# MoE slots filled by an indirect DMA from a DRAM copy of the normed rows, in place of a selection matmul

## The chip, the cores and the metric

One core of a Trainium2 chip runs the program. The metric is device time in microseconds of one execution. The kernel before takes 1042.7 us, the median of 3 runs (1040.01 to 1045.47).

## The reference, cut to what matters

One inference step of two layers over 320 token rows of 1024 features (256 of a new stream, 64 of a running one). Layer 0 uses differential attention, layer 1 forgetting attention; each ends with a mixture of experts (MoE), all in float32. Only the MoE bears on this change:

```python
def hier_moe(t, w_group, b_group, w_expert, b_expert, w_gate, w_up, w_down):
    # one of 4 groups per token, then the 2 best of its 4 experts: gates is (n, 16), 2 nonzero a row
    ...
    for e in range(N_EXPERTS):                       # 16 experts
        hid = jax.nn.silu(t @ w_gate[e]) * (t @ w_up[e])      # (1024, 512) each
        y = y + gates[:, e:e + 1] * (hid @ w_down[e])         # (512, 1024)
    return y
```

`t` is the RMS-normed residual. The weights of one layer's experts are 16 x 3 matrices of 2 MB.

## The kernel before, in words

Rows lie on partitions in three tiles of 128 (the last has 64 real rows). `x` is the residual, `h2` the normed rows that enter the MoE. Semaphores written out by hand set the order on every engine; each engine runs its instructions in program order.

**Routing.** PE computes the router's logits from `h2T` (L1291), VectorE (DVE) picks two experts per row in a chain of some 20 small dependent operations (L1773 to L1788) that ends in the 0/1 matrix `sel`. PE sums `sel` over earlier rows (L1316 to L1326), so each token gets a rank inside its expert. Each expert has CAP = 64 slots. `build_pick` (L1792) compares ranks with 1..64 and makes `pick`, the 0/1 selection matrix (token row x slot) of four experts; its first half is ready before its second (`pick_ready`). `stay_busy(bank, n)` (L971) issues n float32 matmuls of 128x256 on constants, each two instructions, whose result nobody reads.

**Gather.** Experts are worked on in MPAIRS = 8 pairs, two experts of 64 slots filling 128 partitions. `gather(i)` (L1329) multiplies `pick` by the rows: ScalarE (ACT) has split `h2` into a rounded part `h2_hi` (L887) and DVE into the rest `h2_lo` (L1758), and 12 matmuls of 128x512 per pair add both over three tiles. ACT and DVE copy the result to `x_slots` (L897, L1825), `transpose_slots` (L1344) turns it, and both copy it to `xT` (`slots_T`).

**A pair's work on PE**, in this order (L1411 to L1444): `into(i, "g", 0)`, the gate product (32 matmuls); `gather(i + 1)`; `into(i, "u", 1)`, the up product (32); `back(i - 1, (0,))`; `transpose_slots(i + 1)`; four transposes of `hid`; `back(i - 1)` for the other tiles, which scatters the previous pair's outputs through `pickT` and which DVE adds to `x` (L1848); `slots(i + 1)`, which transposes `pick` and picks the gates; `down(i)`, the down product (32).

**Weights.** SyncE (SP) loads the experts' weights in units of 1 MB, 12 for a pair and 96 for a layer, each half of a matrix, in the order in which PE uses them (`load_experts`, L481). There are 15 places for a unit: w_raw (6), w_more (4), w_extra (5). `plan()` (L109) gives each unit a place, and SP waits at L470 until the unit that held it before has been used (`units_used`). In layer 0 the loads of four units of layer 1's input projection (fox_w_in) stand in the same queue before pair 6's down weights (L485 to L487), and fewer places are open to the last 28 units (L149 to L150).

**GpSimd (POOL)** issues the small loads, the stores of keys and values, and computes the inverse roots of the norms (`rms`, L551). In the MoE it has nothing to do.

The overflow branch (more than 64 tokens at an expert) is not entered with these inputs.

Of the kernel before, what the change touches and what calls it, by code (L numbers as in the profile page):

```python
# [22 lines left out]
F32 = mybir.dt.float32  # L23
F32R = mybir.dt.float32r
# [5 lines left out]
P = 128  # L30
# [33 lines left out]
BACK = [3, 0, 5]  # L64

# [4 lines left out]
C_WIDTH = C_PRIO + EXPERTS + 1  # L70
# [5 lines left out]
def constants():  # L76
# [11 lines left out]
    c[:, C_PRIO:C_PRIO + EXPERTS] = np.arange(EXPERTS, 0, -1)  # L88
    dist = np.zeros((P, BIAS), np.float32)
# [72 lines left out]
def build(nc, A):  # L162
    with ExitStack() as ctx:
# [124 lines left out]
        const_r = sb("const_r", [P, 3 * P], F32R, offset=gain_at + 4 * D)  # L288
        before_r, ones_r = const_r[:, 0:P], const_r[:, 2 * P:3 * P]
# [5 lines left out]
        h2_lo = sb("h2_lo", [P, TILES, D], F32R, offset=h_at)  # L295
        h2_hi = sb("h2_hi", [P, TILES, D], F32R, offset=qk_at)
# [34 lines left out]
        def link(eng, which, ins):  # L331
# [19 lines left out]
            sq1=3, rstd1=3, h_ready1=3, tr1=6, ev1=6, h2hi=4, h2lo=3, logits=1, logit_sb=2, gexp=2, selected=1, ranks=2,  # L351
            routed=1, pick_ready=5, gathered=16, slots_act=8, slots_dve=8, slots_tr=16, x_act=8, x_dve=8, pT_done=8, pickT_ready=8, slot_gated=8, silu_done=8,
# [170 lines left out]
        def _(pool):  # L523
# [35 lines left out]
            for l in range(2):  # L559
# [89 lines left out]
                rms(B, "sq1", "rstd1")  # L649

# [11 lines left out]
        def _(act):  # L662
# [9 lines left out]
            for l in range(2):  # L672
# [213 lines left out]
                for t in range(TILES):  # L886
                    A_(h2_hi[:, t, :], h2[:, t, :], ACT.Copy).then_inc(L["h2hi"], 1)  # L887
                A_(const_r[:, :], cst[:, C_BEFORE:C_BEFORE + 3 * P], ACT.Copy).then_inc(L["h2hi"], 1)
# [5 lines left out]

                def copy_slots(i):
                    act.wait_ge(L["gathered"], B["gathered"] + 2 * i + 1)
                    A_(x_slots[:, 0:F], ps[:, 5, :], ACT.Copy).then_inc(L["slots_act"], 1)  # L897
# [17 lines left out]
                copy_slots(0)  # L915
                slots_T(0)
                copy_pickT(0)
                for i in range(MPAIRS):
# [5 lines left out]
                    if i + 1 < MPAIRS:  # L924
                        copy_slots(i + 1)
                        slots_T(i + 1)
                    elif l == 0:

                        split_hi(IN[1][0])
                        split_hi(IN[1][1])  # L930
# [31 lines left out]
        def _(pe):  # L962
# [66 lines left out]
            for l in range(2):  # L1029
# [286 lines left out]
                for t in range(TILES):  # L1316
                    out = ps[:, 7, EXPERTS * t:EXPERTS * (t + 1)]
                    if t == 0:
                        pe.wait_ge(L["h2hi"], B["h2hi"] + 4)
# [7 lines left out]
                pe.wait_ge(L["h2lo"], B["h2lo"] + TILES)  # L1327

                def gather(i):  # L1329

                    pe.wait_ge(L["pick_ready"], B["pick_ready"] + (1 if i == 0 else i // 2 + 2))
                    if i >= 3:
                        pe.wait_ge(L["x_added"], B["x_added"] + 3 * (i - 2))
                    elif i >= 1:
                        pe.wait_ge(L["x_act"], B["x_act"] + i)
                        pe.wait_ge(L["x_dve"], B["x_dve"] + i)
                    cols = slice(i % 2 * P, i % 2 * P + P)
                    for c in range(2):
                        for t in range(TILES):
                            mm(ps[:, 5 + c, :], pick[:, t, cols], h2_hi[:, t, c * F:(c + 1) * F], start=(t == 0), stop=False)  # L1340
                            ins = mm(ps[:, 5 + c, :], pick[:, t, cols], h2_lo[:, t, c * F:(c + 1) * F], start=False, stop=(t == TILES - 1))  # L1341
                        ins.then_inc(L["gathered"], 1)
# [596 lines left out]
```

## Time and profile before

| | |
|---|---|
| median of 3 runs | 1042.7 us |
| the profiled execution | 1042.3 us, its span 1040.5 us |
| PE busy | 974.9 us, 94% of the span, 4789 matmuls |
| DVE, ACT, POOL busy | 434.9, 312.9, 113.6 us |
| chain that ended last | PE 85%, DVE 7%, ACT 3%, DMA 2% |
| of it the gather's two lines, L1340 and L1341 | 3% and 2% |
| DMA | 260.30 MB, mean 250 GB/s, of which SP's queue 242.64 MB |

The span is one execution. "Busy" is the time in which an engine ran an instruction; for PE, ends are modelled, so a busy PE need not be at its peak. The chain is followed back from the last instruction: at each step to what released it. DMA share is the mean busy share of 16 DMA engines. A row of the chain reads: start in us, duration in us, what.

### The profile page before, as it was taken

Reading aid. Unit: us, or ns where it says so; the run is one execution under the profiler, and the core shown is the slowest. Engines: PE = TensorE matmul, PEld = TensorE weight load, DVE = VectorE, ACT = ScalarE, POOL = GpSimd, SP = SyncE. Lnnn points to the kernel's source line nnn. Section 1 sums busy time; section 2 is a strip of 40 time slices with the busy share of each in tenths; the row PEclk is TensorE's granted clock in tenths of the full one; section 3 lists DMA queues with packets and bytes.
Section 4 is the critical chain, followed back from the end, with each engine's and each line's share of the span. In section 5 each row is a group of like instructions: output and inputs, shape, how many; then the busy total and the mean of one; then the engine's idle time right before and its main releaser. Section 6 shows DMA issues by size and latency. Waiting matters only on the chain.

```text
span 1040.5 us, 12144 instructions
## 1 busy us (share of the span) xinstructions
PE 974.9 (94%) x4789; PEld 609.8 (59%) x4789; DVE 434.9 (42%) x883; ACT 312.9 (30%) x612; POOL 113.6 (11%) x148
## 2 busy tenths in 40 slices
PE   4999999898999999988989999999798999999997
PEld 3777666686444444433767777776687444444443
DVE  4666467435122312227366525465625122213223
ACT  4544667323111111124244433343313111111110
POOL 5234123200000000001213310100000000000000
PEclk9999989899999999999899999999799999999999
DMA  9735612534999999997233521311555899999991
GB/s 294 267 122 176 196 43 60 196 149 186 368 421 421 421 421 420 357 420 265 81 122 102 192 80 31 107 45 52 204 232 231 328 420 419 421 422 420 420 414 58
DMA packets 53339, 260.30 MB, mean 250 GB/s; under 512 B 5088, under 2 KB 5328, under 8 KB 28704
## 3 DMA queue, kind: packets, MB, share of 16 engines
q1 hardware_dynamic: 47824, 242.64, 59.0%
q0 software_dynamic: 5456, 16.83, 5.4%
q8 instruction: 42, 0.69, 0.3%
q14 instruction: 17, 0.14, 0.0%
HBM read 252.88 MB, written 6.57 MB: 249 GB/s over the span
## 4 chain that ended last, share of the span: by engine, by line
PE 85%; DVE 7%; ACT 3%; DMA 2%; issue 1%; POOL 1%; SPq 0%; DVEq 0%; POOLq 0%
PE ps L1375 21%; PE ps L1391 11%; PE ps L967 7%; PE ps L968 6%; PE ps L969 6%; PE ps L1340 3%; PE ps L1341 2%; PE ps L1404 2%; PE ps L1020 2%; PE ps L1021 2%; PE ps L1196 2%; PE ps L1405 2%; PE ps L1136 2%; PE ps L1192 2%; PE ps L1350 1%; PE ps L1122 1%
## 5 line engine op out<-in xcount | busy, mean ns | idle before, releaser
L1375 PE MATMUL ps<-w_raw,xT 128*64 128x512 f32 x408 | 174.1, 594 | 0.4 <-issue 0.4
L1375 PE MATMUL ps<-w_extra,xT 128*64 128x512 f32 x376 | 131.5, 594 | 4.0 <-DMA w_raw<-in_moe_w_gate 1.3
L1491 DVE TENSOR_TENSOR w_lo<-w_raw,w_hi 128x2048 fp32r<-128x2048 f32 x36 | 82.1, 2288 | 44.6 <-ACT w_hi L670 44.5
L967 PE MATMUL ps<-w_hi,hT_hi 128*128 128x512 f32 x224 | 94.7, 423 | 3.8 <-DVE w_lo L1491 3.1
L1391 PE MATMUL ps<-w_raw,hidT 128*64 128x512 f32 x216 | 96.0, 595 | 0.0
L968 PE MATMUL ps<-w_lo,hT_hi 128*128 128x512 f32 x224 | 90.2, 403 | 0.0
L969 PE MATMUL ps<-w_hi,hT_lo 128*128 128x512 f32 x224 | 90.1, 402 | 0.0
L1375 PEld LDWEIGHTS ps<-w_extra,xT 128*64 128x64 f32 x376 | 40.8, 137 | 82.3 <-issue 82.3
L1375 PE MATMUL ps<-w_more,xT 128*64 128x512 f32 x240 | 88.4, 593 | 0.0
L670 ACT ACTIVATE w_hi<-w_raw 128x2048 fp32r<-128x2048 f32 x36 | 68.4, 1910 | 42.0 <-PE ps L1021 39.3
L1391 PE MATMUL ps<-w_extra,hidT 128*64 128x512 f32 x184 | 71.1, 595 | 0.0
L1848 DVE TENSOR_TENSOR x<-x,ps 128x1024 f32<-128x1024 f32 x48 | 57.0, 1219 | 12.6 <-PE ps L1405 12.6
L1825 DVE COPY x_slots<-ps 128x512 f32<-128x512 f32 x16 | 11.1, 692 | 118.5 <-PE ps L1341 118.5
L1843 DVE TENSOR_TENSOR y_lo<-ps,y_hi 128x512 fp32r<-128x512 f32 x32 | 22.1, 692 | 90.7 <-ACT y_hi L913 90.6
L1375 PEld LDWEIGHTS ps<-w_raw,xT 128*64 128x64 f32 x408 | 53.0, 137 | 10.3 <-issue 10.3
L1375 PEld LDWEIGHTS ps<-w_more,xT 128*64 128x64 f32 x240 | 27.2, 137 | 53.7 <-issue 53.7
L1872 DVE SCALAR_TENSOR_TENSOR hid<-hid,slot_gate,ps 128x512 f32<-128x512 f32 x16 | 12.0, 747 | 103.9 <-PE ps L1375 103.9
L967 PEld LDWEIGHTS ps<-w_hi,hT_hi 128*128 128x128 f32 x224 | 43.4, 194 | 15.2 <-DVE w_lo L1491 3.5
L901 ACT ACTIVATE xT<-ps 128x512 f32<-128x512 f32 x16 | 9.6, 598 | 134.7 <-PE ps L1350 134.7
L1391 PE MATMUL ps<-w_more,hidT 128*64 128x512 f32 x112 | 49.7, 595 | 0.1
L969 PEld LDWEIGHTS ps<-w_hi,hT_lo 128*128 128x128 f32 x224 | 43.3, 193 | 10.3
L968 PEld LDWEIGHTS ps<-w_lo,hT_hi 128*128 128x128 f32 x224 | 43.5, 194 | 8.3
(290 smaller groups left out, 1771.1 us busy)
## 6 DMA issues: line engine op xcount, KB each, us to landing
w_extra<-in_moe_w_up SPq DMA_DIRECT2D x28, 1024.0 KB, 13.0
w_raw<-in_moe_w_gate SPq DMA_DIRECT2D x27, 1024.0 KB, 10.6
w_raw<-in_moe_w_down SPq DMA_DIRECT2D x27, 1024.0 KB, 11.2
w_raw<-in_moe_w_up SPq DMA_DIRECT2D x24, 1024.0 KB, 12.4
w_extra<-in_moe_w_down SPq DMA_DIRECT2D x23, 1024.0 KB, 13.2
w_extra<-in_moe_w_gate SPq DMA_DIRECT2D x19, 1024.0 KB, 11.7
w_more<-in_moe_w_gate SPq DMA_DIRECT2D x18, 1024.0 KB, 12.8
w_raw<-in_fox_w_in SPq DMA_DIRECT2D x16, 1024.0 KB, 5.4
```

Of the source, the lines that this page charges most:

```text
L670: A_(w_hi[:, U.hslot, :], w_raw[:, U.slot, :], ACT.Copy).then_inc(hi_ready, 1)
L967: mm(out, a_hi, b_hi, start=start, stop=False)
L968: mm(out, a_hi, b_lo, start=False, stop=False)
L969: return mm(out, a_lo, b_hi, start=False, stop=stop)
L1020: mm(acc(b, t), a_hi[:, kb, ts], hi[:, k, :], start=(kb == 0), stop=False)
L1021: ins = mm(acc(b, t), a_hi[:, kb, ts], lo[:, k, :], start=False, stop=(kb == KB - 1))
L1340: mm(ps[:, 5 + c, :], pick[:, t, cols], h2_hi[:, t, c * F:(c + 1) * F], start=(t == 0), stop=False)
L1375: ins = mm(ps[j * CAP:(j + 1) * CAP, bank, :], xT[:, i % 2, kb, j * CAP:(j + 1) * CAP], buffer(U.slot)[:, k * F:(k + 1) * F], start=(kb == ...
L1391: ins = mm(ps[j * CAP:(j + 1) * CAP, 3 + c, :], hidT[:, fb, j * CAP:(j + 1) * CAP], buffer(U.slot)[:, k * D + c * F:k * D + (c + 1) * F], ...
L1491: v.tensor_tensor(w_lo[:, U.slot, :], w_raw[:, U.slot, :], w_hi[:, U.hslot, :].bitcast(F32), ALU.subtract).then_inc(lo_ready, 1)
L1843: v.tensor_tensor(y_lo[:, cs], ps[:, 3 + c, :], y_hi[:, cs].bitcast(F32), ALU.subtract).then_inc(L["y_lo"], 1)
L1848: v.tensor_tensor(x[:, t, :], x[:, t, :], ps[:, BACK[t]:BACK[t] + 2, :].rearrange("p b n -> p (b n)"), ALU.add).then_inc(L["x_added"], 1)
```

## The change: what it does

Per layer, POOL stores the three tiles of `h2` to a DRAM buffer `h2_rows` when each is normed. Constants get a column pair per tile with the value 383 - row. `row_sums(i)` multiplies `pick` by them (3 matmuls, 2 columns), so that each slot gets 383 minus its token's row, or 0 when it is empty; DVE turns that into an integer row number (383 for an empty slot; that row of the padded tile is zero). POOL then gathers 128 rows of 4 KB from `h2_rows` into `x_slots` by one indirect DMA for each pair. `h2_hi`, `h2_lo`, the 12 matmuls, and the copies to `x_slots` go. `transpose_slots(i + 1)` moves into the middle of `down(i)`. Ahead of the first pair two `stay_busy(4, 8)` are put around `slots(0)`.

```diff
+    c[:, C_ROW:C_ROW + 2 * TILES:2] = NO_ROW - (np.arange(TILES)[None] * P + i[:, None])   # NO_ROW = 383
...
+        rows_r = sb("rows_r", [P, TILES, 2], F32R)
+        slot_row = sb("slot_row", [P, 2], I32)
+        h2_rows = [nc.dram_tensor(f"h2_rows{i}", (TILES * P, D), F32, kind="Internal").ap() for i in range(2)]
-        h2_lo = sb("h2_lo", [P, TILES, D], F32R, offset=h_at)
-        h2_hi = sb("h2_hi", [P, TILES, D], F32R, offset=qk_at)
...                                                             GpSimd
                 rms(B, "sq1", "rstd1")
+                for t in range(TILES):
+                    pool.wait_ge(L["h_ready1"], B["h_ready1"] + t + 1)
+                    pool.dma_start(h2_rows[l][t * P:(t + 1) * P, :], h2[:, t, :]).then_inc(L["h2_stored"], 16)
+                pool.wait_ge(L["h2_stored"], B["h2_stored"] + 16 * TILES)
+                for i in range(MPAIRS):
+                    pool.wait_ge(L["slot_rows"], B["slot_rows"] + i + 1)
+                    if i == 0:
+                        pool.wait_ge(L["ranks"], B["ranks"] + 2)
+                    else:
+                        pool.wait_ge(L["slots_tr"], B["slots_tr"] + 2 * i)
+                    pool.indirect_dma_start(x_slots[:, :], None, h2_rows[l][:, :], bass.IndirectOffsetOnAxis(ap=slot_row[:, i % 2:i % 2 + 1], axis=0)).then_inc(L["rows_landed"], 16)
...                                                             ScalarE
-                for t in range(TILES):
-                    A_(h2_hi[:, t, :], h2[:, t, :], ACT.Copy).then_inc(L["h2hi"], 1)
+                A_(rows_r[:, :, :].rearrange("p t n -> p (t n)"), cst[:, C_ROW:C_ROW + 2 * TILES], ACT.Copy).then_inc(L["consts_r"], 1)
...
-                copy_slots(0)
+                copy_pickT(0)
                 slots_T(0)
...
-                    if i + 1 < MPAIRS:
-                        copy_slots(i + 1)
-                        slots_T(i + 1)
...
                     if i + 1 < MPAIRS:
                         copy_pickT(i + 1)
+                        slots_T(i + 1)
...                                                             TensorE
-                def gather(i):
+                def row_sums(i):
                     pe.wait_ge(L["pick_ready"], B["pick_ready"] + (1 if i == 0 else i // 2 + 2))
...
-                            mm(ps[:, 5 + c, :], pick[:, t, cols], h2_hi[:, t, c * F:(c + 1) * F], start=(t == 0), stop=False)
-                            ins = mm(ps[:, 5 + c, :], pick[:, t, cols], h2_lo[:, t, c * F:(c + 1) * F], start=False, stop=(t == TILES - 1))
+                    out = ps[:, ROWS_BANK[min(i, 1)], 0:2]
+                    for t in range(TILES):
+                        ins = mm(out, pick[:, t, i % 2 * P:i % 2 * P + P], rows_r[:, t, :], start=(t == 0), stop=(t == TILES - 1))
+                    ins.then_inc(L["row_sums"], 1)
                 def transpose_slots(i):
-                    pe.wait_ge(L["slots_act"], B["slots_act"] + i + 1)
-                    pe.wait_ge(L["slots_dve"], B["slots_dve"] + i + 1)
+                    pe.wait_ge(L["rows_landed"], B["rows_landed"] + 16 * (i + 1))
+                    if i >= 2:
+                        pe.wait_ge(L["x_added"], B["x_added"] + 3 * (i - 1))
...
                 def down(i):
                     pe.wait_ge(L["hT_copied"], B["hT_copied"] + i + 1)
                     for half in range(2):
+                        if half == 1 and i + 1 < MPAIRS:
+                            transpose_slots(i + 1)
...
-                gather(0)
+                row_sums(0)
+                stay_busy(4, 8)
+                slots(0)
+                stay_busy(4, 8)
                 transpose_slots(0)
-                slots(0)
...
                     into(i, "g", 0)
                     if i + 1 < MPAIRS:
-                        gather(i + 1)
+                        row_sums(i + 1)
...
                     if i + 1 < MPAIRS:
-                        transpose_slots(i + 1)
+                        pe.wait_ge(L["slot_rows"], B["slot_rows"] + i + 2)
...                                                             VectorE
-                low_parts(0)
-                low_parts(1)
...
-                low_parts(2)
...
                 build_pick(0)
+                def slot_rows(i):
+                    dve.wait_ge(L["row_sums"], B["row_sums"] + i + 1)
+                    v.tensor_scalar(slot_row[:, i % 2:i % 2 + 1], ps[:, ROWS_BANK[min(i, 1)], 0:1], -1.0, float(NO_ROW), ALU.mult, ALU.add).then_inc(L["slot_rows"], 1)
+
+                slot_rows(0)
```

On DVE `slot_rows(i + 1)` takes the place of `copy_slots(i + 1)`, and `slots_T(i + 1)` moves behind `take_gates(i + 1)`.

## Rows read from the trace of the kernel before

**Rows 1.** The page: busy tenths in 40 slices of 26 us, PE and DMA.
```profile
PE   4999999898999999988989999999798999999997
DMA  9735612534999999997233521311555899999991
```

**Rows 2.** Windows, two pairs: us; busy PE, PEld, DVE, ACT, POOL; PEclk, DMA share, GB/s.
```profile
343.72:372.54 28.82, 28.82 (x140) 13.15 (x138) 7.29 (x11) 4.08 (x7) 0.00 (x0) 1.00 1.01 421
...
861.68:890.49 28.81, 28.81 (x141) 13.16 (x138) 7.22 (x10) 4.08 (x7) 0.00 (x0) 1.00 1.01 420
```

**Rows 3.** DMA by queue, 8 to 30 us: packets, MB, share of 16 engines.
```profile
q1 hardware_dynamic: 2458, 4.92, 62.0%
q0 software_dynamic: 910, 2.84, 39.8%
```

**Rows 4.** The chain of waits, one pair of layer 0: the gather's first matmul, then up.
```profile
290.74 0.43 PE ps L1340
...
293.71 7.02 PE ps L1375 x32
```

**Rows 5.** The chain of waits, end of the MoE of layer 0.
```profile
460.45 11.11 DMA w_extra<-in_moe_w_up
...
478.86 7.07 PE ps L1391 x32
```

**Rows 6.** Windows in pair 5 of layer 0, where DMA drops.
```profile
422.00:424.00 2.00, 2.00 (x12) 0.58 (x10) 0.09 (x1) 0.00 (x0) 0.00 (x0) 1.00 0.60 246
424.00:426.00 2.00, 2.00 (x12) 0.72 (x10) 0.00 (x0) 0.00 (x0) 0.00 (x0) 1.00 0.42 53
426.00:428.00 2.00, 2.00 (x12) 0.70 (x10) 0.69 (x1) 0.60 (x1) 0.00 (x0) 1.00 0.74 283
```

**Rows 7.** Window in which layer 1's last weights arrive.
```profile
1014.00:1016.00 2.00, 2.00 (x12) 0.62 (x10) 0.00 (x0) 0.00 (x0) 0.00 (x0) 1.00 0.33 131
```

**Rows 8.** The chain of waits, end of the MoE of layer 1.
```profile
1019.55 0.43 PE ps L1404
...
1023.08 7.07 PE ps L1391 x32
```

**Rows 9.** Timeline ahead of layer 0's first pair: start, us, engine, line.
```profile
239.84 1.96 PE L1294 MATMUL ps<-w_router,h2T 128*128 128x20 f32 x16
240.77 2.36 DVE L1758 TENSOR_TENSOR h_lo<-h,h_hi 128x1024 fp32r<-128x1024 f32 x2 [5.32 <-ACT h_hi L887]
241.65 4.56 PE L975 MATMUL ps<-cst 128*128 128x256 f32 x20
243.04 0.21 DVE L1773 TENSOR_TENSOR router<-ps,b_router 128x60 f32<-128x60 f32 x1
...
247.77 0.21 DVE L1787 TENSOR_TENSOR sel<-router,cst 128x48 fp32r<-128x48 f32 x1
...
248.73 0.48 PE L1325 MATMUL ps<-sel,const_r 128*128 128x16 f32 x3
...
249.34 1.03 DVE L1799 TENSOR_TENSOR pick<-router,cst 128x384 fp32r<-128x384 f32 x2
...
252.73 0.21 DVE L1821 TENSOR_TENSOR gates_hl<-router,gates_hl 128x48 fp32r<-128x48 f32 x1
...
255.46 1.13 PE L1350 MATMUL ps<-cst,x_slots 128*128 128x128 f32 x8 [0.88 <-DVE x_slots L1825]
...
257.42 3.65 PE L1375 MATMUL ps<-w_raw,xT 128*64 128x512 f32 x16 [0.19 <-issue]
```

**Rows 10.** Window within it.
```profile
250.00:254.00 4.00, 3.96 (x11) 3.18 (x12) 2.56 (x14) 0.60 (x1) 0.00 (x0) 0.58 0.00 0
```

**Rows 11.** DMA issues: queue, count, KB each, median us from issue to landing.
```profile
w_raw<-in_fox_w_in SPq DMA_DIRECT2D x16, 1024.0 KB, 5.4
...
gain<-in_norm_mix POOLq DMA_DIRECT2D x1, 512.0 KB, 12.3
...
mask<-in_c_mask POOLq DMA_DIRECT2D x1, 480.0 KB, 3.8
```

More of the change, by code:

```diff
@@ L64 @@
 BACK = [3, 0, 5]
+ROWS_BANK = [3, 2]
 C_ID, C_IOTA, C_TRI, C_BEFORE, C_AFTER, C_ONE = (i * P for i in range(6))
@@ L69 @@
 C_PRIO = C_VALID + TILES
-C_WIDTH = C_PRIO + EXPERTS + 1
+C_ROW = C_PRIO + EXPERTS
+NO_ROW = TILES * P - 1
+C_WIDTH = C_ROW + 2 * TILES
 KEYS = [128, 256, 576]
@@ L350, in build @@
             o_hi=6, o_lo=6, out_done=2, low_out_moved=1, x_mid=3,
-            sq1=3, rstd1=3, h_ready1=3, tr1=6, ev1=6, h2hi=4, h2lo=3, logits=1, logit_sb=2, gexp=2, selected=1, ranks=2,
-            routed=1, pick_ready=5, gathered=16, slots_act=8, slots_dve=8, slots_tr=16, x_act=8, x_dve=8, pT_done=8, pickT_ready=8, slot_gated=8, silu_done=8,
+            sq1=3, rstd1=3, h_ready1=3, tr1=6, ev1=6, consts_r=2, h2_stored=48, logits=1, logit_sb=2, gexp=2, selected=1, ranks=2,
+            routed=1, pick_ready=5, row_sums=8, slot_rows=8, rows_landed=128, slots_tr=16, x_act=8, x_dve=8, pT_done=8, pickT_ready=8, slot_gated=8, silu_done=8,
             hid_done=8, hT_done=8, hT_copied=8, y0_done=16, y_hi=16, y_lo=16, back_done=24, x_added=24)
@@ L885, in _ @@
                 copy_h2T(2)
-                for t in range(TILES):
-                    A_(h2_hi[:, t, :], h2[:, t, :], ACT.Copy).then_inc(L["h2hi"], 1)
-                A_(const_r[:, :], cst[:, C_BEFORE:C_BEFORE + 3 * P], ACT.Copy).then_inc(L["h2hi"], 1)
+                A_(const_r[:, :], cst[:, C_BEFORE:C_BEFORE + 3 * P], ACT.Copy).then_inc(L["consts_r"], 1)
+                A_(rows_r[:, :, :].rearrange("p t n -> p (t n)"), cst[:, C_ROW:C_ROW + 2 * TILES], ACT.Copy).then_inc(L["consts_r"], 1)
                 act.wait_ge(L["logit_sb"], B["logit_sb"] + 1)
@@ L923, in _ @@
                     A_(hid[:, :], ps[:, 0, :], ACT.Silu).then_inc(L["silu_done"], 1)
-                    if i + 1 < MPAIRS:
-                        copy_slots(i + 1)
-                        slots_T(i + 1)
-                    elif l == 0:
+                    if l == 0 and i == MPAIRS - 1:
                         split_hi(IN[1][0])
@@ L1318, in _ @@
                     if t == 0:
-                        pe.wait_ge(L["h2hi"], B["h2hi"] + 4)
+                        pe.wait_ge(L["consts_r"], B["consts_r"] + 2)
                     for s in range(t):
@@ L1357, in slots @@
                         pe.wait_ge(L["routed"], B["routed"] + 1)
+                        pe.wait_ge(L["pick_ready"], B["pick_ready"] + 2)
                     else:
@@ L1453, in _ @@
                         t, half = divmod(i, 2)
[L1454 removed]
+                        pe.wait_ge(L["x_added"], B["x_added"] + 3 * MPAIRS)
                         for k in range(4):
@@ L1858, in _ @@
                     if i + 1 < MPAIRS:
-                        copy_slots(i + 1)
+                        slot_rows(i + 1)
                     if l == 0 and i == MPAIRS - 2:
@@ L1880, in _ @@
                         take_gates(i + 1)
+                        slots_T(i + 1)
                 if l == 0:
@@ L1890, in _ @@
                 with dve.If(flag_v > 0):
-                    for t in range(TILES):
-                        v.tensor_tensor(h2[:, t, :], h2_hi[:, t, :].bitcast(F32), h2_lo[:, t, :].bitcast(F32), ALU.add).then_inc(OV[l]["over_done"], 1)
                     v.tensor_scalar(t16, pos, float(CAP), None, ALU.is_gt).then_inc(OV[l]["over_done"], 1)
-                    dve.wait_ge(OV[l]["over_done"], 4)
+                    dve.wait_ge(OV[l]["over_done"], 1)
                     v.tensor_tensor(over_gate[:, :, :], gate16, t16, ALU.mult).then_inc(OV[l]["over_done"], 1)
                     with dve.Fori(0, EXPERTS) as e:
-                        dve.wait_ge(OV[l]["over_done"], e + 5)
+                        dve.wait_ge(OV[l]["over_done"], e + 2)
                         v.tensor_copy(over_col[:, :], over_gate[:, :, bass.ds(e, 1)].rearrange("p t e -> p (t e)")).then_inc(OV[l]["over_done"], 1)
-                        dve.wait_ge(OV[l]["over_done"], e + 6)
+                        dve.wait_ge(OV[l]["over_done"], e + 3)
                         for t in range(TILES):
```

32 lines of the change are left out of this document (2 added, 30 removed).

## The prediction

> **What bounds the kernel now.** I read the page's slices first [rows 1]. PE is at 9 or 10 tenths almost everywhere, so at first sight the kernel is bound by TensorE and each matmul taken away is a gain. The second row says otherwise: in two stretches, slices 11 to 19 and 32 to 39, the two MoE stages, DMA stands at 9 as well. I then took windows of one pair of experts [rows 2]. The reader is to see two full resources at once: a pair takes 28.82 us in either layer, PE busy in all of it, and the DMA engines have share 1.01 at 420 to 421 GB/s. A pair needs 12 units of 1 MB = 12.58 MB, at 421 GB/s 29.9 us. So PE eats a pair in 28.8 us and DMA brings one in 29.9 us; PE lives on the 15 places that were full when the stage began.
>
> Third, the chain of waits at the end of layer 0's MoE [rows 5]. Its piece of 11.11 us is not PE work: a load is issued at 460.45, lands at 471.56, and PE goes on from there. Layer 0's MoE is bound by DMA at its end already, since four units of the next projection stand in its queue. In layer 1 the chain is PE to the last [rows 8], but the last weights have been moved only at about 1014.7 (share 0.33 of the window from 1014) [rows 7], for matmuls that run from 1023. Its cover is thin.
>
> **The sum.** The profiled execution took 1042.3 us, 0.4 under the median of 1042.7; I sum against 1042.3.
>
> *PE's work in a pair.* The gather's 12 matmuls go: from 290.74 to the first up matmul at 293.71, 2.97 us [rows 4]. Three matmuls of 2 columns come; three small ones of the ranks took 0.48 [rows 9], so I take 0.4. A pair is then 28.82 - 2.97 + 0.4, about 26.3 us of PE; 7 gathers in the loop give 18 us a layer. That is what TensorE has less to do, and not yet what the kernel gains.
>
> *DMA's work in a pair.* Each gather brings 128 rows of 4 KB, 0.524 MB. At 421 GB/s that is 1.245 us, and a pair takes 31.1 us of DMA. PE at 26.3 outruns that by 4.8 us a pair; 15 places of 2.49 us are 37 us. So PE leads in the first pairs and starves from about pair 5 on, and in both layers the MoE ends by: when the stream of weights starts, plus its bytes over 421 GB/s, plus PE's work behind the last units. The first gather lies ahead of the stream, in a window where DMA moves nothing [rows 10]; 7 lie in it: 3.67 MB, **8.7 us a layer**. No row shows an indirect DMA. From below its price is 0, if the weights do not feel it. From above I take twice the price, 17.4 us a layer, if rows fetched one by one use the engines half as well. The nearest rows are the kernel's start, where both queues moved data: shares of 62.0% and 39.8%, together 101.8% of 16 engines [rows 3]. They share the engines, with no second set; 7.76 MB in those 22 us are 353 GB/s with shorter packets than here, by which a gather costs 1.49 and a layer 10.4 us. I stay at 8.7, since 4 KB rows are nearer to the weights' long ones.
>
> The Trainium skill (DMA: Bandwidth & Descriptors, section Issuing engines are not separate DMA queues) states that DMAs issued from several engines run on the same 16 engines and interleave, so that a second issuer saves only issue time. By that rule the term is 8.7 or more; without it the term would be 0. Rows 3 agree, at 101.8%.
>
> *Stores of h2.* 1.57 MB per layer, 3.7 us of DMA, between the norm and the first pair. The stream stands still there later on (0 GB/s from 250 to 254) [rows 10], which hides them. Without that cover they cost 3.7 us. The last tile must be in DRAM when the row numbers are ready at about 249.5. It is normed before its logits start at 239.84 [rows 9]; at 3.8 to 12.3 us for a transfer of this size [rows 11] it has landed, at the slow end just so.
>
> *A drop that closes.* In layer 0 DMA moved 246, 53 and 283 GB/s in three windows of 2 us from 422 [rows 6]: 1.16 MB where 2.53 fit, 3.2 us lost, because SP waited for places that PE frees in pair 5. PE will be there some 10 us sooner and DMA will be behind: **-3.2 us**.
>
> *Waits in the loop.* POOL asks for the rows when DVE has the numbers, just after the gate product; PE waits for them in the middle of down. From the first up matmul to there it is 28.8 less gate (7), gather (3) and half of down (3.5), some 15 us. Behind that wait on PE stand down's second half and everything after it, on POOL only later gathers and the next layer's norm. A transfer of this size landed in 3.8 us alone and in 12.3 us in a full queue [rows 11]; what POOL needs for 128 row addresses no row shows, between 0 and 8.5 (their difference), and I take 2. Hidden at 6 to 14 us; were it 20 us, the 4.8 us by which PE outruns DMA would absorb nearly all. Copies by ACT and DVE go or move to engines that are busy 4 and 7 us of 28.8 [rows 2]: nothing.
>
> *The head of each MoE.* DVE starts the routing chain at 243.04 only because two low parts (240.77, 2.36 us) hold it; the logits were done at 241.80 [rows 9]. Their removal brings the chain 1.1 us forward. `sel` is ready at 246.9 and the second half of `pick` at 249.2. PE's row sums end near 249.1, and then come: stay_busy, 16 instructions at 4.56/20 = 0.228 us [rows 9], 3.65 us, to 252.8; slots, 0.83 us (256.59, the transposes' end, to 257.42), to 253.6; again 3.65, to 257.2. The gates, at 252.94 before, are there at 252.1. Transposes start at 257.2 where they started at 255.46, and the weights 1.96 us behind them as now, at 259.2: **+1.8**. The rows, asked for at 249.5, land at 255.3 by the estimate of 2 + 3.8, under stay_busy. The clock adds a term: from 250 to 254 PE was granted 0.58 [rows 10], the 1.2 GHz level for some 3.4 of 4 us, after an idle stretch from 246.2 to 248.0. If this falls on stay_busy it costs 1.7 more. The idle stretch is now 0.7 us, but 2 us of sparse work follow; I take half, 0.9. **Head: +2.7**, bounds 1.8 and 3.6, the same in layer 1.
>
> The Trainium skill (TensorE: Matmul & The Clock Gate, Part 1: The HAM clock gate) says that throttled is the default and activity releases it. By it the shorter idle speaks for the lower bound, 1.8; by the row as it stands 3.6.
>
> *Layer 0:* the end moves with the stream, 8.7 - 3.2 + 2.7 = **+8.2 us**. *Layer 1:* a unit alone takes 5.4 us [rows 11], 2.5 of it transfer; with half of the rest behind the data, the last down unit landed at 1016.1 and the last up unit four units, 10 us, earlier: 1006.1. Later by 8.7, 1014.8; then half of up 3.5, then 3.53 (1019.55 to 1023.08) and down 7.07 [rows 8]: 1028.9 where it was 1030.15. So -1.3 and the head's 2.7, **+1.4 us**. Attention has no changed work. Together +9.6: 1051.9, I forecast **1052 us**. PE's 36 us are not lost but turned into waits for weights.
>
> **Rivals.**
> *The gathers ride free, and it gets faster.* If the weights' stream keeps its pace, both terms of 8.7 go: 1052 - 17.4 = 1034.5. For it: PE has 36 us less to do, and layer 1's chain is all PE. Against it: shares of 1.01 leave nothing free. Its point: with 14 gathers in the two streams, no slower than before needs under 0.56 us a gather, and 0.5% faster under 0.22. 0.12, and 0.10 more for a part of the price, near 1044.
> *Late rows.* POOL needs so long for an indirect DMA, or it is served so late, that PE stands at the first transposes and, over and over, in down. 3 us later in each head make 1058; it decides from 8 us between the row numbers and the landing. For it: 12.3 us in a full queue; against it: idle engines at the head. 0.15.
> *Dear rows.* Twice the engine time per gather: 1052 + 17.4 = 1069. 0.08.
> *The forecast*, PE's saving turned into waits for weights and the gathers' bytes paid in full: 0.55.
>
> **How the numbers follow.** About 0.5%, 5.2 us, is what a measurement of this kernel can tell from no change. Below 1037.5 lies most of the first rival: faster 0.10. Between 1037.5 and 1047.9 lie its partial case and the forecast's low edge: same 0.20. Slower 0.70. The range reaches down to 1041, where a gather costs about 0.5 us, and up to 1063, which is 1.49 us a gather (3.4 more), both heads at their upper bound (1.8 more) and late rows (6 more).
>
> **What would show it.** Right: pairs 1 to 4 at about 26.3 us and later ones at 31; DMA share 1.0 to the end of both MoE stages, without the drop; PE waiting for weight loads in pairs 5 to 7; layer 0's weights ending some 8 us later than now and layer 1's stage ending with PE's last down close behind its last weights; the first gate product about 9.7 us after the row numbers; rows landing 6 to 14 us after they are asked for. Wrong: a stream that moves more than 421 GB/s with the gathers in it, pairs at an even 26 us throughout, or waits in down on the rows instead of on weights.

## The result, and the profile after

The changed kernel takes 1050.84 us (median of 7 runs, 1048.1 to 1054.49) against 1043.11 us for the kernel before on the same chip (7 runs, 1040.01 to 1045.47): ratio 1.0084, 95% interval 1.0062 to 1.0105. It is slower by 0.8%, forecast 1052. TensorE is busy 14.7 us less (960.2 us, 974.9 before), although the four new `stay_busy(4, 8)` take 18.0 us of it, and the kernel ends 7.7 us later.

The page after: busy tenths in 40 slices, the two queues, the chain by engine, the row gather's issues (busy us, mean ns | idle before, releaser).

```profile
PE   4999998899999998868889999999799999998886
DMA  9735521545999999998232530211558699999995
...
q0 software_dynamic: 8624, 28.37, 8.0%
...
PE 72%; DMA 17%; DVE 6%; ACT 3%; issue 1%; POOL 1%; SPq 0%; DVEq 0%; POOLq 0%
...
L665 POOL DMA_INDIRECT x_slots<-h_rows,slot_row x16 | 15.5, 968 | 379.3 <-DVE slot_row L1802 348.8
```

The DMA row still stands at 9 through nearly all of both MoE stages; what fell is the PE row at the end of both: 6 in slice 18 where [rows 1] had 8, and 8, 8, 8, 6 in the last four where it had 9, 9, 9, 7. DMA's share of the chain went from 2% to 17%: waits for weights took the place of matmuls. The queue issued by POOL moved 28.37 MB (16.83 before).

The chain of waits of layer 0's MoE (start us, us, what), with one pair before the starving and the waits behind it:

```profile
286.08 6.87 PE ps L1377 x32
292.95 0.42 PE ps L1341 x3
293.37 7.02 PE ps L1377 x32
...
308.14 1.09 PE ps L1351 x8
...
312.81 6.87 PE ps L1377 x32
...
379.66 27.54 DMA w_raw<-in_moe_w_up
...
418.80 19.36 DMA w_extra<-in_moe_w_up
...
443.98 20.83 DMA w_extra<-in_moe_w_gate
...
468.64 11.09 DMA w_extra<-in_moe_w_up
...
487.02 7.07 PE ps L1395 x32
```

Between gate product (L1377, 286.08) and up product (293.37) stand three small matmuls of 0.42 us where [rows 4] had a gather of 2.97. From gate to gate it is 312.81 - 286.08 = 26.73 us. From 379.66 on, four loads are pieces of the chain: the weights are late, as only once in [rows 5]. In layer 1, where [rows 8] had none, there are three, the last of them:

```profile
997.57 29.94 DMA w_raw<-in_moe_w_up
1027.51 0.14 issue
1027.65 3.65 PE ps L1377 x16
...
1034.81 7.07 PE ps L1395 x32
```

Windows after (columns as in [rows 2]): a pair that PE leads, two stretches of starving, and the last of layer 1's weights.

```profile
338.00:364.00 26.00, 26.00 (x129) 11.08 (x127) 7.64 (x11) 3.38 (x6) 0.94 (x1) 1.00 1.02 421
416.00:442.00 26.00, 22.27 (x106) 8.23 (x103) 3.04 (x8) 2.39 (x4) 1.13 (x1) 1.00 1.02 415
442.00:468.00 26.00, 16.86 (x77) 8.07 (x78) 6.80 (x10) 3.08 (x6) 0.00 (x0) 0.87 1.02 414
...
1034.00:1036.00 2.00, 2.00 (x10) 0.83 (x10) 2.00 (x2) 0.00 (x0) 0.00 (x0) 1.00 0.83 344
1036.00:1038.00 2.00, 2.00 (x12) 0.72 (x10) 0.28 (x1) 0.00 (x0) 0.00 (x0) 1.00 0.15 61
```

With PE busy 26.00, 22.27 or 16.86 of 26 us, DMA has the same share and 414 to 421 GB/s. The drop to 53 GB/s of [rows 6] is gone. Layer 1's last weights move until 1036 to 1038, and PE's last down product begins at 1034.81; in [rows 7] and [rows 8] the stream was finished some 8 us ahead of the last down product.

The head of layer 0's MoE (timeline; in brackets the idle time before and its releaser):

```profile
240.53 1.96 PE L1302 MATMUL ps<-w_router,h2T 128*128 128x20 f32 x16
...
242.53 0.22 DVE L1769 TENSOR_TENSOR router<-ps,b_router 128x60 f32<-128x60 f32 x1 [8.08 <-PE ps L1302]
...
249.71 5.34 PE L983 MATMUL ps<-cst 128*128 128x256 f32 x16
...
249.88 0.16 DVE L1802 TENSOR_SCALAR slot_row<-ps 128x1 int32<-128x1 f32 x1 [0.16 <-PE ps L1341]
...
250.87 1.05 POOL L665 DMA_INDIRECT x_slots<-h_rows,slot_row  x1 [15.59 <-DMA h_rows<-h]
...
254.70 0.59 PE L1363 MATMUL ps<-gates_hl,pick 128*128 128x32 f32 x3
...
255.52 3.62 PE L983 MATMUL ps<-cst 128*128 128x256 f32 x16
...
258.98 1.04 PE L1351 MATMUL ps<-cst,x_slots 128*128 128x128 f32 x8
...
260.85 3.65 PE L1377 MATMUL ps<-w_raw,xT 128*64 128x512 f32 x16 [0.83 <-ACT xT L912]
```

The stage in milestones, us of each profiled execution. Head: from the third tile's logits to the first gate product. Stage: from there to the start of the last down product. Stream: from the first load after the head to the last weights' landing.

| | head, layers 0 and 1 | stage | stream |
|---|---|---|---|
| before | 17.6, 17.6 | 221.4, 216.6 | 220.4, 206.2 |
| after | 20.3, 20.3 | 226.1, 215.2 | 225.1, 214.1 |

The profiled execution of after took 1054.07 us (span 1052.3), 11.8 more than that of before: heads +5.5, stages +4.7 and -1.4, attention between the layers +2.3, and +0.7 ahead of the first MoE and behind the last. The last two terms hold no changed work but the stores of `h2`; the experiments come back to them.

### The profile page after: what moved, and what is told of

It reads as the page before. It is cut to its first block, busy times and chain, and to the rows that moved or that the text cites. A ratio compares the mean times of both kernels' runs of the same rounds, so it can differ in the third digit from the quotient of the medians.

```text
span 1052.3 us, 11980 instructions
## 1 busy us (share of the span) xinstructions
PE 960.2 (91%) x4709; PEld 595.5 (57%) x4709; DVE 420.8 (40%) x877; ACT 297.4 (28%) x592; POOL 132.1 (13%) x170
## 2 busy tenths in 40 slices
DMA packets 56507, 271.83 MB, mean 258 GB/s; under 512 B 5440, under 2 KB 5680, under 8 KB 31872
## 3 DMA queue, kind: packets, MB, share of 16 engines
q0 software_dynamic: 8624, 28.37, 8.0%
## 4 chain that ended last, share of the span: by engine, by line
PE 72%; DMA 17%; DVE 6%; ACT 3%; issue 1%; POOL 1%; SPq 0%; DVEq 0%; POOLq 0%
PE ps L1377 15%; DMA w_raw<-in_moe_w_up 11%; PE ps L1395 7%; PE ps L975 7%; PE ps L977 6%; PE ps L976 6%; DMA w_extra<-in_moe_w_up 3%; PE ps L983 3%; PE ps L1028 2%; DMA w_extra<-in_moe_w_gate 2%; PE ps L1029 2%; PE ps L1204 2%; PE ps L1144 2%; PE ps L1200 2%; PE ps L1408 1%; PE ps L1130 1%
## 5 line engine op out<-in xcount | busy, mean ns | idle before, releaser
L1377 PE MATMUL ps<-w_raw,xT 128*64 128x512 f32 x408 | 175.1, 595 | 1.7 <-ACT xT L912 1.7
L1377 PE MATMUL ps<-w_extra,xT 128*64 128x512 f32 x376 | 132.3, 595 | 15.7 <-DMA w_raw<-in_moe_w_up 8.1
L1395 PE MATMUL ps<-w_raw,hidT 128*64 128x512 f32 x216 | 99.4, 605 | 0.0
L1377 PE MATMUL ps<-w_more,xT 128*64 128x512 f32 x240 | 89.1, 594 | 6.0 <-DMA w_more<-in_moe_w_gate 2.5
L1377 PEld LDWEIGHTS ps<-w_extra,xT 128*64 128x64 f32 x376 | 40.6, 137 | 92.1 <-issue 92.1
L1395 PE MATMUL ps<-w_extra,hidT 128*64 128x512 f32 x184 | 74.1, 606 | 8.9 <-DMA w_raw<-in_moe_w_down 8.9
L665 POOL DMA_INDIRECT x_slots<-h_rows,slot_row x16 | 15.5, 968 | 379.3 <-DVE slot_row L1802 348.8
L1377 PEld LDWEIGHTS ps<-w_more,xT 128*64 128x64 f32 x240 | 27.4, 137 | 58.3 <-issue 58.2
L1377 PEld LDWEIGHTS ps<-w_raw,xT 128*64 128x64 f32 x408 | 52.2, 137 | 10.8 <-issue 8.7
L939 ACT ACTIVATE hidT<-ps 128x512 f32<-128x512 f32 x16 | 9.6, 599 | 147.9 <-PE ps L1438 147.9
L1395 PEld LDWEIGHTS ps<-w_extra,hidT 128*64 128x64 f32 x184 | 21.0, 139 | 42.5 <-issue 40.6
## 6 DMA issues: line engine op xcount, KB each, us to landing
w_raw<-in_moe_w_up SPq DMA_DIRECT2D x24, 1024.0 KB, 20.6
w_extra<-in_moe_w_gate SPq DMA_DIRECT2D x19, 1024.0 KB, 20.8
```

Source lines behind the costliest of these rows:

```text
L1377: ins = mm(ps[j * CAP:(j + 1) * CAP, bank, :], xT[:, i % 2, kb, j * CAP:(j + 1) * CAP], buffer(U.slot)[:, k * F:(k + 1) * F], start=(kb == ...
L1395: ins = mm(ps[j * CAP:(j + 1) * CAP, 3 + c, :], hidT[:, fb, j * CAP:(j + 1) * CAP], buffer(U.slot)[:, k * D + c * F:k * D + (c + 1) * F], ...
```

## The experiments

Theory A, the prediction's: the MoE ends with the stream of weights; PE's saving became waits, and each gather costs the stream its bytes. Rivals: the gathers are much dearer than their bytes, or free; PE still sets the end; the fillers (`stay_busy`) in the head are a loss of their own. "Stage", "head" and "stream" are those of the table above. All changes are to the kernel after, unless it says otherwise. "Ratio" is to the kernel before, run beside it on the same chip. The experiments ran on four chips (e1, e2, e4, e5; e3, e6, e8, e9; e9b, f3, m1; m3). After itself was run with none of these groups, so a difference to it of a few us in the medians is weaker evidence than the lengths of the stages in the profiles.

**e1: one gather a layer.** Gathers 1 to 7 are left out, so these pairs compute on pair 0's rows.

```diff
+                    if i == 0:
                         pool.indirect_dma_start(x_slots[:, :], None, ...
-                    pe.wait_ge(L["rows_landed"], B["rows_landed"] + 16 * (i + 1))
+                    pe.wait_ge(L["rows_landed"], B["rows_landed"] + 16)
```

> From the changed kernel; per layer only the first of 8 indirect gathers is issued (the one ahead of the weights' stream), pairs 1 to 7 transpose the rows of pair 0. It leaves out 7 x 0.524 MB of DMA in each weight stream and nothing else. Theory A (the gathers' bytes delay the weights one for one, 1.245 us each at 421 GB/s): each stream 8.7 us shorter, 17.4 us in all, about 1033.5 us where the changed kernel takes 1050.8. Theory B (the bytes ride free; the loss sits in the two heads, +2.7 each, and in attention's scatter): no change, 1050 to 1051.

1030.7 us, ratio 0.9879 (0.9846 to 0.9913). Stages 217.1 and 206.1: 9.0 and 9.1 us less than after, **1.29 and 1.30 us for each gather left out**. The head, with its fillers, is unchanged (20.3). So the row gathers in the stream are the larger part of the loss: without them the new kernel beats the old by 1.2%.

**e2: each gather twice**, the second into a spare buffer.

```diff
+                    if i:
+                        pool.indirect_dma_start(x_twice[:, :], None, ...).then_inc(L["rows_landed"], 16)
-                    pe.wait_ge(L["rows_landed"], B["rows_landed"] + 16 * (i + 1))
+                    pe.wait_ge(L["rows_landed"], B["rows_landed"] + 16 * (2 * i + 1))
```

> From the changed kernel; each of the gathers 1 to 7 of a layer is issued twice, the second into a spare buffer that nobody reads. Theory A: 8.7 us more a layer, 17.4 in all, about 1068 us. Theory B (bytes ride free): no change. Theory C (POOL's work on 128 row addresses, about 1 us in the trace, or late rows at PE are what costs): under 2 us more, as long as the rows land before the middle of down.

1066.76 us, ratio 1.0241 (1.0202 to 1.0279). Stages 235.3 and 224.5: +9.2 and +9.3, 1.31 and 1.33 each. Zero, one and two gathers a pair lie on a line. The bytes of one over 421 GB/s are 1.245 us: a gather is neither free nor twice as dear. Where the 4 to 7% over its bytes go, no run separates.

**e4: 2.7 us of PE work more a pair.** If the stream sets the end, this is free.

```diff
                         row_sums(i + 1)
...
+                    if i + 1 < MPAIRS:
+                        stay_busy(1, 6)
                     into(i, "u", 1)
```

> From the changed kernel; 12 float32 matmul instructions of 128x256 on constants are put before the up product of pairs 0 to 6, 12 x 0.228 = 2.7 us each, 38 us of TensorE in all: about what the removed selection matmul took. Theory A (both MoE stages are bound by the weights' arrival, PE at 26.7 us a pair against 31.1 us of DMA): PE goes to 29.5 a pair, still under 31.1, so 0 to 1.5 us more, 1051 to 1052.5 us. Theory D (TensorE's work still counts): up to 38 us more, about 1089 us.

1060.76 us, ratio 1.0167 (1.0133 to 1.0202): 9.9 more than after, where A said 0 to 1.5. A's number failed. From gate product to gate product it is now 29.44 us, all of it PE:

```profile
349.35 6.87 PE ps L1377 x32
...
356.64 2.70 PE ps L983 x12
359.34 7.02 PE ps L1377 x32
...
378.79 6.87 PE ps L1377 x32
```

I had compared paces: PE at 29.4 us a pair is still quicker than DMA at 31.1. But PE has the lead of 15 full places at the start, and a stage has only 8 pairs. What counts is the totals. PE's work in a stage, never starved, is about 202.9 us (e1's layer 1, 206.1 less 3.2 of waiting in its last pair, whose first gate product to last down product took 20.6 us where its matmuls alone take 17.4). Seven fillers of 2.7 are 18.9: 221.8. The stage of after lasts 226.1 in layer 0 and 215.2 in layer 1. So by the larger of PE's total and the stream's: 226.1 and 221.8; measured 226.5 and 221.7. The stream is 1.1 us longer in layer 0 and the same in layer 1 (226.2 and 214.3). So PE had slack in after, 23 us in layer 0 and 12 in layer 1, and no more: with over 12 us of PE work added to a stage the rival that PE sets the end becomes true of layer 1. The stages account for 7.0 of the 9.9 us; the intervals of the two ratios leave 3 to 15.

**e5: from the kernel before, a thin gather by matmul.** For pairs 1 to 7 only 2 of the 12 gather matmuls are done (the rounded part of the first tile), the rest of the sum is left out. PE gets the saving, the stream gets no gather.

```diff
-                        for t in range(TILES):
...
+                        if i:
+                            ins = mm(ps[:, 5 + c, :], pick[:, 0, cols], h2_hi[:, 0, c * F:(c + 1) * F], start=True, stop=True)
+                        else:
+                            for t in range(TILES):
...
```

> From the kernel before; for pairs 1 to 7 the selection matmul is cut from 12 to 2 matmuls (one tile, one part), no DMA is added. It leaves out most of the gather's arithmetic. About 2.4 us less TensorE work a pair, 33.6 us in all. Theory A: layer 0 was bound by DMA and gains only the 3.2 us in which its stream stood still, layer 1 gains until its own last weights bind, at most 10 us: 1030 to 1033 us. Theory D (TensorE's work counts in full): about 1009.5 us.

1024.08 us, ratio 0.9827 (0.9795 to 0.986): 18.0 less than before, more than forecast. Stages 217.3 and 206.3, that is -4.1 and -10.3. In layer 0 the bytes are unchanged, and 4.1 us is what closing the drop of [rows 6] gives. In layer 1 the stage now ends with the stream (205.4). PE saved 14 times 2.3 us, 32; without any price 14.3 of them reach the end of the two stages.

The interval of the ratio leaves 14.6 to 21.4 us, so the stages don't cover the whole gain of the medians. The two profiled executions differ by 4.0 us outside heads and stages: 2.6 in attention, 1.3 behind the last down product. Windows from the last down product of layer 0 to the third tile's logits of layer 1, one for each kernel: before, after, e5.

```profile
478.86:788.79 309.93, 292.34 (x1486) 221.16 (x1486) 160.67 (x321) 116.29 (x223) 45.74 (x52) 0.96 0.36 124
```

```profile
487.02:799.24 312.22, 293.86 (x1487) 221.48 (x1486) 160.80 (x321) 116.12 (x223) 47.49 (x55) 0.95 0.36 123
```

```profile
474.60:782.01 307.41, 289.33 (x1486) 219.63 (x1486) 160.72 (x321) 116.23 (x223) 45.65 (x52) 0.97 0.36 126
```

The same 1486 matmuls (one record more in after) take 309.9 us at a mean granted clock of 0.96, 312.2 at 0.95 and 307.4 at 0.97. By the clock records of each trace the 1.2 GHz level was held for 27.3, 30.7 and 20.5 us of it. The other readable profiles show the same: from e1, 307.9 us with 20.5 at that level, to m1 and m3, 312.9 and 313.0 with 34.1; all 13 together give about 0.4 us for each us at 1.2 GHz. The kernels differ there only in the stores of `h2`, and these cost at most 0.3 to 0.5 us (e2 310.3 against before 310.0, both with 27.3 us low; e1 307.9 against e5 307.4, both with 20.5). So most of the 2.3 us between the profiles of before and after is the clock of the execution. The runs of one kernel show it too: of the 29 of before beside f3 the fastest took 1036.72 us at a mean granted clock of 0.978 and the slowest 1045.75 at 0.971. Why e5's median gains 3.7 us more than its stages remains open: its four runs have a mean clock of 0.970 to 0.973, no higher than most of before's.

**e3: no fillers in the head.**

```diff
                 row_sums(0)
-                stay_busy(4, 8)
                 slots(0)
-                stay_busy(4, 8)
                 transpose_slots(0)
```

> From the changed kernel; both stay_busy(4, 8) ahead of the first pair are taken out, nothing else. The first rows landed at 255.3 in the profile of the changed kernel, and PE turned to the transposes at 259.0. Theory A (PE's own filler work holds the head, and a head's delay moves the stream and the end one for one): each head 3.6 us shorter, less at most 1.7 if the gate product then starts at the 1.2 GHz level: 1043.5 to 1047.5 us where the changed kernel takes 1050.8. Theory E (the filler is free since the rows come no sooner, or the clock it keeps is worth as much): no change.

1049.23 us, ratio 1.0083 (1.0057 to 1.0109), no different from after's 1.0084. The rival that the two fillers together are worth what they cost was right. The head is 18.8 and 17.8, 1.5 and 2.5 shorter; the first pair takes 27.8 and 28.0 instead of 25.1. From the logits to the last down product e3 is 1.1 and 0.5 us longer than after. Windows around the first gate product (257.2 here, 260.85 in after), first e3, then after:

```profile
257.00:263.00 6.00, 5.80 (x16) 1.94 (x18) 0.10 (x1) 0.45 (x1) 0.00 (x0) 0.52 0.00 0
259.00:265.00 6.00, 6.00 (x22) 2.03 (x20) 0.00 (x0) 0.00 (x0) 0.00 (x0) 0.69 0.14 20
```

```profile
257.00:263.00 6.00, 5.17 (x28) 3.48 (x29) 0.69 (x1) 1.88 (x2) 0.00 (x0) 1.00 0.00 0
259.00:265.00 6.00, 5.17 (x29) 2.61 (x29) 0.69 (x1) 1.88 (x2) 0.00 (x0) 1.00 0.00 0
```

Without fillers TensorE waits for the rows and then starts its first gate product at the 1.2 GHz level (a granted clock of 0.52 in the window). The first place comes free when half of that product is done, 6.4 us after its start where after needs 3.7, so the next load starts 25.3 and 24.5 us after the logits, against 24.0 with fillers. It is the stream, not the first product, that must start early.

**e8: e3, with each tile of `h2` stored as soon as it is normed** (before, three norms, then three stores).

```diff
-                rms(B, "sq1", "rstd1")
                 for t in range(TILES):
+                    rms(B, "sq1", "rstd1", (t,))
                     pool.wait_ge(L["h_ready1"], B["h_ready1"] + t + 1)
                     pool.dma_start(h2_rows[l][t * P:(t + 1) * P, :], h2[:, t, :]).then_inc(L["h2_stored"], 16)
```

> Like the run without stay_busy, and each store of h2 is issued as soon as its tile is normed; in the changed kernel the first two stores waited behind the third tile's inverse root on POOL, and the first gather waited for a store, 0.8 us in layer 0 and 1.9 us in layer 1 past the row numbers. Theory A: the gathers are issued that much earlier: 2.7 us in all below the run without stay_busy. Rival: the last store lands no sooner, since the weights share the engines: same as that run.

1047.4 us, ratio 1.005 (1.0025 to 1.0074), 1.8 less than e3 where 2.7 were expected; the intervals of the two overlap. The first load comes 24.4 and 22.6 us after the logits, 0.9 and 1.9 sooner than in e3. The stores land in 8.1 us (median; 12.1 in e3), and the first gather waits for the row numbers alone: it is issued 0.84 and 0.80 us behind them, in e3 2.04 and 0.88.

**e6: empty slots fetch nothing.**

```diff
-    bass.IndirectOffsetOnAxis(ap=slot_row[...], axis=0))
+    bass.IndirectOffsetOnAxis(ap=slot_row[...], axis=0), bounds_check=TILES * P - 2, oob_is_err=False)
```

> From the changed kernel; the indirect DMA gets a bound of 382 on the row number, so that empty slots (row 383) fetch nothing: 384 of 1024 slots, if the routing leaves 640 of 1024 filled. Their slots keep old rows, with a gate of zero. Theory A: in-stream gathers carry 37% less, 14 x 0.49 us = 6.8 us less, about 1044 us. Theory F (what a gather costs is its 128 descriptors or POOL's work, not its bytes): no change.

1047.06 us, ratio 1.0046 (1.0025 to 1.0066), against an expected 1044. The packets of e6:

```profile
DMA packets 56507, 268.69 MB, mean 257 GB/s; under 512 B 6208, under 2 KB 6448, under 8 KB 31872
...
q0 software_dynamic: 8624, 25.22, 7.4%
```

3.15 MB less, 768 rows of 4 KB out of 2048. But the packets are 8624 as before, and those under 512 B rose from 5440 to 6208, by exactly 768: a skipped row is still a packet, a short one. If the 14 gathers in the stream hold 7/8 of the skipped bytes, these are 6.5 us at 421 GB/s; the streams are 2.3 and 1.0 us shorter. Half of the saving came. That the short packets eat the rest is a guess that no run tested.

**e9: gather 1 issued in the head**, right behind gather 0, into a buffer of its own, so that 6 and not 7 lie in the stream.

```diff
+                row_sums(1)
...
+                pe.wait_ge(L["slot_rows"], B["slot_rows"] + 2)
...
+                    pool.indirect_dma_start((x_ahead if i == 1 else x_slots)[:, :], None, ...
```

> From the changed kernel; the row numbers of pair 1 are made in the head too and its gather is issued right behind the first, into a second buffer, where the DMA engines are idle. Same work, same bytes. Theory A (only bytes inside the weights' stream cost): 1.3 us less a layer, 2.6 in all, about 1048 us. Rival (a gather costs wherever it is, or its latency counts): no change or slower.

1052.03 us, ratio 1.0102 (1.0081 to 1.0124), the ratio without the execution told of next. The one execution that was profiled took 3219.74 us. In it the gate and up matmuls took 1.92 us each where they take 0.6, at a granted clock of 1.00, while DVE and ACT were as quick as ever; why, nothing here shows. The other four took 1050.13 to 1052.99 us, where 1048 was expected. The kernel was run again on another chip:

> The kernel with pair 1's gather ahead of the stream once more, for a profile that can be read. By its times it gained nothing where 2.6 us were expected. Theory A': the stream is 1.3 us shorter in each layer, and the head is longer by as much, since the second row sum waits for the second half of pick and pushes stay_busy and the gates back. Rival: the stream is no shorter, a gather costs wherever it is. The profile tells which by the time from the first load behind the head to the last weights' landing (225.1 and 214.1 us in the changed kernel).

1047.67 us, ratio 1.0052 (1.0031 to 1.0072). Stages 224.7 and 213.9, streams 223.7 and 212.8: -1.4 and -1.3 us for one gather less in each, about the 1.3 of e1 and e2. But the heads are 20.8 and 22.4 us, +0.5 and +2.1, and that eats the gain, as expected before this run: three more row sums stand ahead of the fillers, and in layer 1 the 1.2 GHz level lay over 6.8 us of the head where it is 3.4 in layer 0. The two intervals of one kernel don't meet; each speaks for its own chip alone, so differences of half a per cent are told only within a group of kernels run together.

**f3: skipped rows, stores tile by tile, one filler** (the first `stay_busy(4, 8)`; the second goes).

> From the changed kernel, all gathers kept: empty slots skipped, the stores of h2 issued tile by tile, and only the first stay_busy(4, 8) left in the head. By the traces skipping took 3.3 us from the two streams. In the head the first weights' place was freed 24.0 us after the third tile's logits; without the second stay_busy PE can transpose when the rows land, some 3 us sooner, if TensorE is still granted 2.4 GHz in the first gate product. Theory A: 1050.0 - 3.3 - 6 = about 1041 us. Rival H (the idle 3 us in front bring the 1.2 GHz level into the first gate product, as without any stay_busy, where its pair took 27.8 us against 25.0): 1045 to 1047 us.

1040.94 us, ratio 0.9984 (0.9966 to 1.0001). The head is 16.9 us in both layers, 3.5 less than after, and the first pair still takes 25.1 in both: the second filler gave nothing that the first had not given. The first load starts 20.6 us after the logits. In the profiles the heads are 6.9 us and the stages 3.0 shorter than after, together the 9.9 by which the medians differ. Three things changed at once here; how the head's 3.5 us divide between filler and earlier stores was not run. Nothing tells f3 from the kernel before: its interval holds 1.

**m1: gathers by DMA only where PE sets the end.** From the kernel before: layer 0 as it was; in layer 1 pairs 1 to 3 by indirect DMA, the others by matmul.

```diff
+BY_DMA = [(), (1, 2, 3)]
...
+                    if i + 1 in BY_DMA[l]:
+                        row_sums(i + 1)
+                    elif i + 1 < MPAIRS:
                         gather(i + 1)
```

> From the kernel before, not from the changed one: layer 0 stays as it was; in layer 1 only pairs 1, 2 and 3 get their rows by indirect DMA (row sums, transposes in the middle of down, DRAM copy stored tile by tile), the other five by the selection matmul. By the profiles PE then needs 216.6 - 3 x 2.1 = 210.4 us from layer 1's first gate product to its last down product, and the weights' stream 206.1 (its length with no gather in it) + 3 x 1.3 = 210.0. Theory A (a MoE stage ends by the later of PE's total and the stream's total, and a gather takes 2.1 us from the one and adds 1.3 to the other): about 6 us faster than before, 1036 to 1038 us. Rival G (the machinery of both ways costs what it saves: the wait of the low parts for the DRAM store in the head, late rows): 1041 to 1044 us.

1038.81 us, ratio 0.996 (0.994 to 0.9979): 3.5 less than before, where A said about 6. Layer 1's stage is 211.2, 5.4 less than before, and layer 0's 221.6 as before. Both heads are 18.5, 0.9 more, also in layer 0, where nothing was changed: in each the 1.2 GHz level lay over 6.8 us, in before over 3.4. So 5.4 - 1.8 = 3.6 us remain, and whether the 0.9 in layer 1 is the change's or the clock's can't be told.

**m3: m1 with pairs 1 to 4, and skipped rows.**

> The kernel of both ways with pairs 1 to 4 of layer 1 by indirect DMA and empty slots skipped. By the sums: PE 216.6 - 4 x 2.1 = 208.2 us from layer 1's first gate product to its last down product, the stream 206.1 + 4 x 0.8 = 209.3; the first kernel of both ways showed 211.2. Theory A: 1 to 2 us below that kernel's ratio of 0.996 to the kernel before, a ratio of about 0.994 to 0.995, some 1037 us. Rival: with the stream and PE this close the ends no longer follow the sums, and it stays at 0.996 or above.

1034.59 us against 1042.81, ratio **0.9924** (0.9899 to 0.995): it beats both kernels. Layer 1's stage is 210.3, its head 18.5. Stages and heads are 4.5 us shorter than before in the profiles and the medians 8.2 apart (the interval leaves 5.2 to 10.5), so part of the gain is not located. Its chain in layer 1, gate products of a pair whose successor is gathered by DMA and of one by matmul, and the end:

```profile
863.48 6.87 PE ps L1420 x32
...
890.21 6.87 PE ps L1420 x32
...
945.76 6.87 PE ps L1420 x32
...
974.59 6.87 PE ps L1420 x32
...
988.07 26.49 DMA w_raw<-in_moe_w_up
...
1021.86 7.07 PE ps L1438 x32
```

26.73 us, then 28.83. One load has come onto the chain, near the end. The stream (209.2 us, 209.3 expected) ends the stage again, while PE's total is 208.2: with four pairs the two are nearly even. Two or five pairs, and a mix in layer 0, were not tried.

## Why the prediction was right, step by step

**What bounds the kernel.** Right. Full DMA under a full PE in [rows 2] was what decided. e5 gives PE nearly the same saving without a byte more and gains 18.0 us (14.3 in the stages); after, with the bytes, loses 7.7.

**PE's work in a pair, "about 26.3 us".** Measured 26.73. Row sums take 0.42 (0.4 predicted), but the transposes, put into the middle of down, take 1.09 where they took 0.88, and down in its two halves 7.16 where it took 7.02. Pairs 0 to 4 have periods of 25.1 and four times 26.7, pair 5 has 30.4 and 30.1 in the two layers, pair 6 in layer 1 31.1, the number predicted; in layer 0 it has 41.7, with the four units of the next projection in its queue.

**"8.7 us a layer" for seven gathers.** The mechanism was right, the size 4 to 7% small: 9.0 to 9.3 by e1 and e2, 1.29 to 1.33 us each in place of 1.245. The price from [rows 3], 1.49, was too dear. The Trainium skill (DMA: Bandwidth & Descriptors, Issuing engines are not separate DMA queues) has it that a second issuer shares the same 16 engines; this case agrees, with 420 GB/s from 980 to 1006 us both in after (share 1.01, gathers in the stream) and in e1 (1.01, none).

**"A drop that closes: -3.2".** Measured 4.1 by e5 in layer 0's stage. With the gathers' 9.0 it is 4.9 net, where the stage grew by 4.7; predicted 5.5.

**"Head: +2.7".** Measured +2.7 in both layers, but by two terms that were each off and cancel; that much is luck. The clock term was put at 0.9, half of 1.7, and was 1.5: the same 16 instructions took 4.99 us in the first `stay_busy`, from start to the next start (249.71 to 254.70), and 3.46 in the second (255.52 to 258.98), with a granted clock of 0.62 in the window from 250 to 254, as 0.58 in [rows 10]. The other steps were put at +1.8 and came to +1.2: each `stay_busy` without the clock's part is 3.46 us in place of 3.65, and the smaller steps give the rest. The routing chain starts 2.00 us after the logits instead of 3.20 (1.2 gained, 1.1 predicted). The lower bound, argued from the shorter idle stretch with the Trainium skill (TensorE: Matmul & The Clock Gate, Part 1: The HAM clock gate), was wrong: the clock fell all the same, and the row was the better guide. So the gate product came 10.8 us behind the row numbers, not 9.7.

**The stores of `h2`.** Their upper bound of 12.3 us to landing was too low: the three take 8.3, 13.0 and 15.5 us in layer 0. The last landed at 250.24, 0.2 us behind the row numbers, and the gather was issued at 250.87, 0.83 behind the numbers, as in e8 where no store is waited for. In layer 1 the gather was issued 1.1 us later than that (810.69, numbers at 808.73). It cost nothing, since in both layers the rows were there before PE had done its fillers (in layer 0 at 255.3, with PE at the transposes from 258.98).

**Rows hidden at 6 to 14 us.** Right. All 16 gathers, issue to landing:

```profile
L665 POOL DMA_INDIRECT x_slots<-h_rows,slot_row x16: 935/940/1132, 250.9 to 991.2; - x16
...
DMA to landing us min/median/max: 4.4/9.0/10.1
```

POOL needs 0.94 us where I took 2 from a range of 0 to 8.5. The rows of the pair shown above landed at 303.37, 4.8 us ahead of their transposes at 308.14, and no wait of PE in down is on rows, so "late rows" is out.

**Layer 0, "+8.2", and layer 1, "+1.4".** From the third tile's logits to the last down product layer 0 grew by 7.5 us, layer 1 by 2.7 - 1.4 = 1.3. Together 8.8 for 9.6 predicted, and 7.7 by the medians.

**"Attention has no changed work."** True but for the stores, and yet its time differed by 2.3 us in the profiles, most of which goes with the clock of the execution. A sum against one profiled execution carries that uncertainty.

**What the prediction missed** is not in its sum but in its reasoning: "DMA brings one in 29.9, PE eats one in 28.8" is a comparison of paces, and e4 shows that with 15 full places and 8 pairs the totals decide. I used totals for the end times, and these came out; in e4's expectation I used paces, and it failed.

## What to carry to other kernels

Where two resources are both full, moving work from one to the other pays only up to the point at which their totals over the stage, prefetched buffers included, are equal. In layer 1 the sums (216.6 - 2.1 a pair against 206.1 + 1.3 a pair) put it at 3 of 8 pairs, at 3 to 4 with empty slots skipped; in layer 0 the stream already ended the stage, and a mix there was not tried. Idle-time fillers ahead of a burst of matmuls must be judged by when the next load can start, and each one by itself. If a transfer is to replace compute, ask first what the engines already move in those same microseconds.

## What was not expected of the hardware

- An indirect DMA of 128 rows of 4 KB costs POOL 0.94 us and lands after 4.4 and 4.9 us on idle engines (the two heads) and after 7.1 to 10.1 us beside a full queue of weights; in the stream it costs 1.29 to 1.33 us, 4 to 7% over its bytes.
- Rows skipped by the bounds check move no data but remain as packets of under 512 B (5440 became 6208, 768 more), and about half of their time came back (3.3 of 6.5 us, e6).
- The time at 1.2 GHz within attention varies from execution to execution of nearly the same instructions, 20.5 to 34.1 us over 13 profiles, and its length with it, 307.4 to 313.0 us. The stretch ahead of the first MoE varies more, 236.3 to 242.9 us, with 6.8 to 27.3 us at 1.2 GHz. What sets it, no run here shows.
